# Layer one's output projection as seven-product pairs of row blocks, with row and weight sums in place

## What is computed

```
out = jnp.concatenate([y_mix, ym], axis=-1) @ w_out        # layer one: (tokens, 1536) @ (1536, 1024)
x = x + _rmsnorm(out, p['g_post'][l])
h = _rmsnorm(x, p['g_pre'][l + 1])                         # what layer two starts from
```

## Time and profile before

| | us |
|---|---|
| median of 3 runs (1755.45 to 1756.52) | 1755.72 |
| the profiled execution's own time | 1758.04 |
| its span in the trace | 1756.3 |
| PE busy | 1741.5 |
| DVE / ACT / POOL busy | 872.8 / 595.0 / 499.3 |
| A's output stage in the trace, 732.35 to 913.53 | 181.18 |

### The profile page before, as it was taken

How to read it: one execution, slowest core, us unless ns; L and a number is a source line. 1 busy time by engine, 2 the same in 40 slices (tenths; PEclk the granted TensorE clock), 3 DMA queues, 4 the chain that set the end, 5 groups by cost and what they waited for, 6 DMA issues and landing times.

```text
span 1756.3 us, 22816 instructions
## 1 busy us (share of the span) xinstructions
PE 1741.5 (99%) x8470; PEld 1353.8 (77%) x8470; DVE 872.8 (50%) x1801; ACT 595.0 (34%) x1445; POOL 499.3 (28%) x539
## 2 busy tenths in 40 slices
PE   9999999999999999999999999999999999999998
PEld 5577766888788888747558888888888888889643
DVE  0444423776666556451333443355335544565775
ACT  1421234564565234311221233432333234533312
POOL 0151100335232012410003543145414643122640
PEclk9999999999999999999999999999999999999999
DMA  8311111246755235541111111323123343745333
GB/s 271 138 61 66 66 45 50 55 151 158 230 171 166 85 100 164 178 147 48 50 58 57 41 48 45 99 88 96 50 73 117 97 148 109 266 146 181 132 108 110
DMA packets 149081, 196.25 MB, mean 112 GB/s; under 512 B 19083, under 2 KB 108171, under 8 KB 148834
## 3 DMA queue, kind: packets, MB, share of 16 engines
q1 hardware_dynamic: 140708, 174.58, 31.3%
q10 hardware_dynamic: 8262, 20.20, 3.3%
HBM read 156.97 MB, written 37.85 MB: 111 GB/s over the span
## 4 chain that ended last, share of the span: by engine, by line
PE 90%; DVE 3%; issue 3%; ACT 1%; DMA 1%; POOL 1%; SPq 0%; DVEq 0%; ACTq 0%; POOLq 0%
PE PS L3547 50%; PE PS L2289 7%; PE PS L2439 6%; PE PS L2079 3%; PE PS L575 3%; PE PS L401 3%; PE PS L2530 2%; PE PS L2115 2%; PE PS L2090 2%; PE PS L296 2%; PE PS L2112 2%; PE PS L925 1%; DVE WK L732 1%; PE PS L918 1%; PE PS L3445 1%
## 5 line engine op out<-in xcount | busy, mean ns | idle before, releaser
L3547 PE MATMUL PS<-HT,RING 128*128 128x258 f32 (+2 forms) x1776 | 445.6, 382 | 0.3 <-ACT WK L3637 0.3
L3547 PEld LDWEIGHTS PS<-HT,RING 128*128 128x128 f32 x1776 | 328.5, 190 | 48.0 <-issue 4.1
L3637 ACT ACTIVATE BIG<-PS 128x256 f32<-128x256 f32 (+2 forms) x140 | 53.7, 384 | 375.2 <-PE PS L3547 375.1
L3547 PE MATMUL PS<-BIG,RING 128*128 128x258 f32 (+1 forms) x656 | 159.7, 382 | 0.9 <-DVE BIG L3731 0.9
L3547 PEld LDWEIGHTS PS<-BIG,RING 128*128 128x128 f32 x656 | 123.0, 190 | 19.1 <-DVE BIG L3731 1.3
L3547 PE MATMUL PS<-BIG,WK 128*128 128x258 f32 (+1 forms) x448 | 113.7, 383 | 0.0
L3547 PE MATMUL PS<-HT,CST 128*128 128x256 f32 (+2 forms) x432 | 110.2, 382 | 0.1
L3547 PEld LDWEIGHTS PS<-BIG,WK 128*128 128x128 f32 x448 | 82.7, 190 | 14.0 <-issue 3.0
L3547 PEld LDWEIGHTS PS<-HT,CST 128*128 128x128 f32 x432 | 79.6, 190 | 11.4 <-DVE BIG L3736 0.9
L575 PE MATMUL PS<-WK,RING 128*128 128x344 f32 x288 | 84.3, 453 | 0.1
L3733 DVE TENSOR_TENSOR BIG<-BIG,PS 128x256 f32<-128x256 f32 (+1 forms) x70 | 29.5, 422 | 103.6 <-PE PS L3547 103.4
(11 more groups left out here) (455 smaller groups left out, 3270.6 us busy)
## 6 DMA issues: line engine op xcount, KB each, us to landing
RING<-in_w_in_a SPq DMA_DIRECT2D x14, 1024.0 KB, 6.7
WK<-in_cache_mem_kv SPq DMA_DIRECT2D x56, 256.0 KB, 5.6
RING<-in_w_kv_b SPq DMA_DIRECT2D x12, 1024.0 KB, 5.2
RING<-in_w_in_b SPq DMA_DIRECT2D x12, 1024.0 KB, 5.3
WK<-in_cache_win SPq DMA_DIRECT2D x40, 256.0 KB, 5.4
RING<-in_w_mkv SPq DMA_DIRECT2D x16, 512.0 KB, 4.9
BIG<-in_x_prompt SPq DMA_DIRECT2D x16, 512.0 KB
BIG<-sample_query SPq DMA_DIRECT2D x28, 256.0 KB, 5.8
```

What stands on the lines that cost most here:

```text
L3547: last = nc.tensor.matmul(PS[:, bank, 0:mid - lo], weight_block(u // 2, s, k), h_block(layer_of(u), u % 2, t, k), start=(k == 0 and j not ...
L3637: nc.scalar.activation(part(u, n2 if j == 0 else n1, lo, mid), PS[:, banks(u)[0], 0:mid - lo], ACT.Copy).then_inc(sig("projections_copied" ...
```

## The change

Layer one's output takes the form that layer two's has. `column_products`, `columns_turn`, `block_products` and `out_pe` go. Each of the four pairs takes seven products of six pieces x 512 columns; the first factor's blocks are the rows of the two token blocks (pieces 0 to 5 and 6 to 11), the second factor's are the weights (pieces 0 to 5 and 6 to 11, two halves of columns). The order of blocks becomes layer two's, with the sample block as number 4.

- Row sums S1 to S4 are made by DVE, mostly in place over the rows they come from (two instructions each, 16 sums).
- Weight sums: T3 and T4 by POOL, T1 and T2 by DVE, six instructions of 128x512 each, mostly in place.
- The results are summed by DVE with `pair_sum_dve` and copied by `pair_copy_act`, as in layer two.
- The sample block is computed by `sample_rows_pe` (12 pieces x 4 strips of 256 columns, bank 6).
- Turns of blocks 7 and 8 move into layer two's slots 3 and 6 (before: block 8's in slot 4); the T sums of layer two's second unit move from slots 5 to 7 to slots 7 to 9. Layer two's first unit waits for seven copied blocks and for each T sum where it needs it.

```diff
+        PAIR_ORDER_A = [(0, 0), (2, 0), (5, 0), (7, 0), (0, 2), (2, 2), (5, 2), (7, 2),
+                        (0, 4), (0, 1), (0, 3), (0, 5), (0, 6),
+                        (2, 1), (2, 4), (2, 3), (2, 5), (2, 6),
+                        (5, 1), (5, 4), (5, 3), (5, 5), (5, 6),
+                        (7, 1), (7, 5), (7, 3), (7, 4), (7, 6)]
...
+            out, x, y, op = {S3: (s3, a11, a21, ALU.subtract), S1: (a21, a21, a22, ALU.add),
+                             S2: (a11, a21, a11, ALU.subtract), S4: (a12, a12, a11, ALU.subtract)}[s]
+            for n in range(2):
+                last = nc.vector.tensor_tensor(out[n], x[n], y[n], op)
...
+        def weight_sum_a(engine, ops, t):
+            if t == T3:
+                engine.wait_ge(*product_done(UA - 1, NPROD - 1))
+                engine.wait_ge(sig("out_weights_loaded").sem, 80)
+                engine.wait_ge(sig("late_weights_loaded").sem, 128)
+            elif t == T1:
+                engine.wait_ge(*weights_a_ready(T3))
+                engine.wait_ge(sig("sample_rows_done").sem, 1)
+            elif t == T2:
+                engine.wait_ge(*weights_a_ready(T1))
+                engine.wait_ge(*pair_product_done("A", OUT_PAIRS[-1], 0))
+            elif t == T4:
+                engine.wait_ge(*weights_a_ready(T2))
+                engine.wait_ge(*pair_product_done("A", OUT_PAIRS[-1], 2))
+            x, y = {T3: (B22, T1), T1: (T1, B11), T2: (B22, T1), T4: (T2, B21)}[t]
+            for k in (0, 1, 5, 2, 3, 4):
+                if t == T4 and k == 2:
+                    engine.wait_ge(*pair_product_done("A", OUT_PAIRS[0], 4))
+                last = ops.tensor_tensor(weight_tile(t, k), weight_tile(x, k), weight_tile(y, k), ALU.subtract)
+            last.then_inc(sig("pair_weights_summed").up(), 1)
...
+        def out_a_pe(pe, free0, free1):
...
+            pair_product(pe, x, p2, 0, early)
+            pair_product(pe, x, p3, 0, early)
+            samples_turned_pe(pe, x)
+            pe.wait_ge(sig("late_weights_loaded").sem, 128)
+            for p in OUT_PAIRS:
+                pair_product(pe, x, p, 0, range(5, 6))
+            pe.wait_ge(sig("small_read").sem, SMP[x]["small"]["sp"])
+            sample_rows_pe(pe, x, range(8))
+            pe.wait_ge(sig("ym_ready").sem, 4)
+            for n, p in enumerate(OUT_PAIRS):
+                pair_product(pe, x, p, 2)
+                value(2 * n)
+                value(2 * n + 1)
+            pair_product(pe, x, p0, 4)
...
+            pair_product(pe, x, p1, 5)
+            block_turn(pe, x, 1)
+            pair_product(pe, x, p1, 6)
+            pair_product(pe, x, p2, 1)
+            pair_product(pe, x, p2, 4)
+            block_turn(pe, x, 2)
+            pair_product(pe, x, p2, 3)
+            block_turn(pe, x, 3)
...
+            pair_product(pe, x, p3, 4)
+            block_turn(pe, x, 6)
+            pair_product(pe, x, p3, 6)
...
+        def out_a_dve(dve, sample_out):
...
+            for n in range(4):
+                value(n)
+            weight_sum_a(dve, nc.vector, T1)
+            value(4)
+            value(5)
+            rows(p0, S3)
+            rows(p0, S1)
+            weight_sum_a(dve, nc.vector, T2)
+            value(6)
+            value(7)
+            rows(p0, S2)
+            rows(p0, S4)
...
+            pair(p1, C21)
+            h_copy_dve(dve, x, 1)
+            block_all_dve(dve, x, 2)
+            pair(p1, C12)
+            block_dve(dve, x, 3)
+            pair(p2, U2)
+            block_norm_dve(dve, x, 3)
+            row_sums_dve_a(dve, p3)
+            block_all_dve(dve, x, 4)
+            h_copy_dve(dve, x, 2)
...
+            h_copy_dve(dve, x, 6)
+            h_copied(dve, 7)
+            h_sum(dve, "B", 0, T1)
+            h_sum(dve, "B", 0, T2)
+            block_dve(dve, x, 7)
+            pair(p3, C12)
+            h_sum(dve, "B", 0, T3)
+            h_sum(dve, "B", 0, T4)
+            block_dve(dve, x, 8)
...
         def stage5_pool(pool):
+            weight_sum_a(pool, nc.gpsimd, T3)
             scale_pair(pool, PA)
             sum_pair(pool, PA)
+            weight_sum_a(pool, nc.gpsimd, T4)
             scale_pair(pool, PA + 1)
...
         def layer_b_dve(dve):
...
+                if x == 1:
+                    block_norm_dve(dve, "A", 7)
+                if x == 3:
+                    block_norm_dve(dve, "A", 8)
                 if x == 4:
+                    h_copy_dve(dve, "A", 7)
+                if x == 7:
                     h_copy_dve(dve, "A", 8)
+                    h_copied(dve, NB)
+                if 7 <= x < 10:
+                    for t in ((T1, T2), (T3,), (T4,))[x - 7]:
                         h_sum(dve, "B", 1, t)
```

More of the change, by code:

```diff
@@ L2350, in row_blocks @@
         def row_blocks(i):
-            first, second = (slice(BLOCKS["B"][j] * P, (BLOCKS["B"][j] + 1) * P) for j in (i + 1, i))
+            first, second = (slice(BLOCKS[j] * P, (BLOCKS[j] + 1) * P) for j in (i + 1, i))
             y, ym = tiles4(0, 1), tiles4(16, 1)
@@ L2429, in pair_product @@
+            u = BLOCKS[i + 1 if s in (A11, A12) else i]
             rows = slice(u * P, (u + 1) * P)
             for k in ks:
[L2431 to L2438 removed]
@@ L2439, in pair_product @@
-                last = nc.tensor.matmul(PS[:, bank, :], x, w, start=(k == 0 and j not in (2, 3, 6)), stop=(k == 3),
+                if x == "A":
+                    y, w = row_tile(i, s, k), weight_tile(t, k)
+                else:
+                    y = row_sum(i, s)[:, k] if s in (S1, S2, S3, S4) else c.src(k if s == A11 else 4 + k, rows.start, rows.stop)
+                    if t in (T1, T2, T3, T4):
+                        w = weight_sum(t)[:, k]
+                    else:
+                        w = c.piece(k if t == B11 else 4 + k)
+                        w = w[:, 512:D] if t == B22 else w[:, 0:512]
@@ L2440, in pair_product, with pair_copied @@
+                last = nc.tensor.matmul(PS[:, bank, :], y, w, start=(k == 0 and j not in (2, 3, 6)), stop=(k == nk - 1),
                                         skip_group_check=True)
-            if ks[-1] == 3:
+            if ks[-1] == nk - 1:
                 last.then_inc(sig("projections_done").up(), 1)
[L2444 to L2452, removed]
+        def pair_copied(x, i):
+            n = 2 * UA if x == "A" else 2 * NUNIT + len(OUT_PAIRS)
+            return sig("projections_copied").sem, n + OUT_PAIRS.index(i) + 1
@@ L2502, in sample_rows_pe, with sample_rows_bank @@
+        def sample_rows_bank(x):
+            return 6 if x == "A" else 7
+        def sample_rows_pe(pe, x, kts):
+            c = OUT[x]
+            if kts[-1] == c.kts - 1:
+                pe.wait_ge(sig("sample_out_read").sem, SMP[x]["order"] + 1)
+            for kt in kts:
                 for q in range(4):
-                    last = nc.tensor.matmul(PS[32 * q:32 * q + NS, 7, 0:256], c.src(kt, T, W),
+                    last = nc.tensor.matmul(PS[32 * q:32 * q + NS, sample_rows_bank(x), 0:256], c.src(kt, T, W),
@@ L2549, in build, with value @@
-        VALUE_SLOTS = {"A": {(0, 6): 0, (0, 7): 1, (0, 9): 2, (0, 10): 3, (1, 5): 4, (1, 6): 5, (1, 8): 6, (1, 10): 7}}
-        TURN_SAMPLES = {"A": 8}
-        def out_pe(pe, x, free0, free1, weights0, weights1):
-            c, order = OUT[x], SMP[x]["order"]
-            slots = VALUE_SLOTS[x]
-            def value(i):
-                def after(kt):
-                    if (i, kt) in slots:
-                        sample_values_pe(pe, x, slots[i, kt])
-                return after
-            def turns(at):
-                def after(kt):
-                    for i in at.get(kt, ()):
-                        block_turn(pe, x, i)
-                return after
-            early, late = range(c.early), range(c.early, c.kts)
-            own, cross = range(c.kts - H), range(c.kts - H, c.kts)
+        def out_a_pe(pe, free0, free1):
+            x = "A"
+            p0, p1, p2, p3 = OUT_PAIRS
+            def value(n):
+                sample_values_pe(pe, x, n)
+            early = range(5)
@@ L2578, in out_pe @@
-            ym = 0
-            pe.wait_ge(sig("ym_ready").sem, ym + 1)
-            pe.wait_ge(*weights1)
-            for i in range(2):
-                block_products(pe, x, i, late, value(i))
-            pe.wait_ge(sig("ym_ready").sem, ym + 4)
-            hold = turns({6: (0,), 11: (1,)})
-            last = value(2)
-            def both(kt):
-                last(kt)
-                if kt == TURN_SAMPLES[x]:
-                    sample_out_pe(pe, x)
-                hold(kt)
-            block_products(pe, x, 2, late, both)
```

493 lines of the change are left out of this document (272 added, 221 removed).

## The result

The changed kernel takes **1759.49 us** (median of 20 runs, 1757.96 to 1764.92), the kernel before 1756.43 (20 runs, 1754.94 to 1758.99). The ratio is 1.0019, with a 95% interval from 1.0012 to 1.0025: 3.1 us slower, a small change, but its interval lies wholly above 1. The forecast was 1.0 us faster. The profiled execution has a span of 1760.4 us and an own time of 1762.27.

What follows compares the result with a forecast made beforehand. TensorE (PE) was taken as the bound, busy 1741.5 of 1756.3 us. Its work falls 19.7 us, waits add 18.7, so 1.0 less: 1754.7 us, own range 1751 to 1758 (chance 0.50), stated range with rivals 1744.5 to 1761.

Steps and rivals of the forecast that it cites:

- PE's work: Layer one's output stage: 168.9 us of PE work removed, 150.0 added, 0.8 for shape changes, so 19.7 less.
- the values: Sample values late on DVE, which loses 13.4 us beside POOL; value 7 ready at 788.8, PE waits 7.9 us.
- U2 of the first pair: This sum comes about 0.4 us late, since two row sums before it run beside T4's second half.
- turn of block 3: PE waits 4.0 us for DVE's copy of block 2, which stands behind the sample block.
- layer two, slots 2 and 3: Start of layer two, from turn 6: DVE needs 14.8 us against PE's 10.4, a wait of 4.4.
- layer two, second unit: Block 8's copy and T1, T2 stand behind slot 6's sum: waits of 1.3 and 0.7, 2.0 us together.
- The clock falls in the pauses: Slower rival, chance 0.09: half clock behind two long pauses costs 5.2 us each, 10.3 more, 1765.0 us.
- row sums at half speed: Slower rival, chance 0.10: strided row sums take twice the time before value 7 and in stall 2, 6 more, 1760.7 us.
- DVE one for one with POOL: Side by side, each DVE instruction with two SBUF inputs starts about every 1.57 us and loses 0.95.
- eight sums at 0.4: At the values: POOL's sum of layer two's first weights, eight short instructions costing DVE 0.4 us each, put at 3.0.
- stall 2: PE's wait at the turn of block 3: DVE's 26.3 us against PE's 22.4, put at 4.0 us.
- The first rival: Faster, chance 0.31: DVE and POOL hardly meet, the values' wait and its 0.4 vanish, 9.3 us less, 1746.4.

Runs made afterwards that it cites:

- e7_u2_first: e5_both with layer two's start reordered (block 8's work and T4 later) and DVE summing U2 of the first pair ahead of two row sums: 1737.54 us, ratio 0.9883.
- e3_fill: Changed kernel with unused matmuls filling PE's pauses ahead of values 6 and 7 and of turn 3, waits kept: 1756.30 us, ratio 1.0002.
- e1_pool_first: Changed kernel with POOL scaling and summing layer two's first weights before T3, not between T3 and T4: 1749.39 us, ratio 0.9958.
- e2_copy_first: Changed kernel with DVE and ACT copying block 2 ahead of the sample block, not behind it: 1753.82 us, ratio 0.9988.
- e4_all_pool: Changed kernel with weight sums T1 and T2 moved from DVE to POOL, none left on DVE: 1763.46 us, ratio 1.0035.
- e5_both: Changed kernel with the edits of e1_pool_first and e2_copy_first together: 1743.07 us, ratio 0.9920.

## Why the prediction was wrong, point by point

e7_u2_first has the same order of work on PE as the changed kernel, with one short pause in the stretch that is compared. Laid beside it, the changed kernel's timeline shows what every pause really cost. The stage's first product and the sixth of layer two's second unit, in e7_u2_first:

```profile
731.79 3.70 PE L2542 MATMUL PS<-BIG 128*128 128x512 f32 x8 [0.51 <-DVE BIG L3877]
...
915.34 1.92 PE L3679 MATMUL PS<-BIG,RING 128*128 128x260 f32 x8
```

and slot 2's pause in the changed kernel:

```profile
911.60 1.89 PE L3682 MATMUL PS<-WK 128*128 128x256 f32 x8
914.88 1.99 PE L3682 MATMUL PS<-HT,RING 128*128 128x256 f32 x8 [1.39 <-ACT BIG L3772]
```

The same stretch takes 183.55 us in e7_u2_first, 206.21 in the changed kernel (732.92 to 939.13) and 202.98 before (732.35 to 935.33, the same product). In e7_u2_first 0.43 of it is idle. At slot 2 the changed kernel needs 3.28 us from start to start for what is 1.73 undisturbed: 1.55 lost, where the trace shows an idle time of 1.39. So each pause costs somewhat more than its idle time, here 0.16. That is how idle time is counted, and no cost of its own: undisturbed, eight such records are shown as 1.89 us long but the next start 1.73 us after them, so an idle time that is counted from their shown end leaves 0.16 out. The prediction's stalls were counted from start to start, and the last column is their like.

| | forecast, us | idle time shown | lost against e7_u2_first |
|---|---|---|---|
| PE's work | -19.7 | | -20.0 |
| the values (4 pauses) | 7.9 | 7.9 | 8.45 |
| U2 of the first pair | 0.4 | 0.75 | 0.8 |
| turn of block 3 | 4.0 | 3.95 | 4.1 |
| layer two, slots 2 and 3 | 4.4 | 3.2 | 3.75 |
| layer two, second unit (2 pauses) | 2.0 | 2.4 | 2.8 |
| clock behind the pauses | 0 | | 3.3 |
| sum | -1.0 | | +3.2 |

The last column is the growth of the distance between equal products of the two traces across each pause, the 0.5 us of e7_u2_first's own pause added at the second unit. PE's work is 202.98 less 183.0 (183.55 without that pause). The sum meets 206.21 - 202.98 = 3.23.

**The step that failed is the clock.** The sum had no term for it. "The clock falls in the pauses" stood as a rival with 0.09, on the ground that "no row shows a pause of this length, so nothing speaks for it but its absence". The mechanism is the rival's: long pauses at the last values and at turn 3, in places and of a total size that the sum had forecast, and the records behind them at the lower level. One detail differs. The rival had one pause of some 4 us before value 6; there were two, 2.59 before value 6 and 3.64 before value 7, and the clock fell within the second (1.00 still for the records of 785.66, which take 0.43). The chance was too low, because the same prediction forecast pauses more than twice as long as the longest that the earlier trace rows showed at 1.00; an untried range is no evidence for either side. Its price was too high: 5.2 us behind each pause, 10.3 in all and 1765.0, where 1.7 and 1.6 were measured. I had priced a whole product at half speed. In the changed kernel the granted clock is 1.00 again from 794.00, at the end of about these eight records, and part of its time at the lower level lay inside the pauses (0.56 in the stretch from 786.00, in which PE was busy for 0.66 us), where it costs nothing. By the right size the rival would have given 1754.7 + 3.3 = 1758.0. Shown by e3_fill, which filled the pauses and gave 3.2 back, and by e1_pool_first and e2_copy_first, each of which gave back its wait and the clock behind it. The waits came to 19.9 us rather than 18.7, and PE's work to 20.0 rather than 19.7. So of the 4.2 us between the forecast (1.0 less) and this stretch (3.2 more) 3.3 are the clock and 0.9 the rest. That 1759.49 lies inside the stated range of 1744.5 to 1761 is luck: its upper end was set by the row sums at half speed, which did not happen, and the clock was left out of it.

The Trainium skill, "TensorE: Matmul & The Clock Gate" (Part 1), has a TensorE that was idle go back to half rate. The windows at 0.56 to 0.61 in and behind the pauses agree, and e3_fill's 1.00 with the pauses filled agrees as well.

**PE's work: right.** 20.0 us less, forecast 19.7.

**The books of two runs.** Ten pauses show 18.3 us of idle time and cost 19.9. With the costs, e1_pool_first should give back 8.45 + 1.7 = 10.1 and gave 10.1, e2_copy_first 4.1 + 1.6 = 5.7 and gave 5.7 at the medians. That both close to 0.1 us is in part luck. In the profiled executions the same stretch is 9.1 and 6.5 us shorter than in the changed kernel (197.14 and 199.71), since the clock's cost behind the pause that stayed was not the same (last section), and in e2_copy_first the waits that stayed were some 0.5 us shorter.

**The values: right in size and cause.** DVE one for one with POOL, 13.7 us lost against 13.4. e1_pool_first takes POOL's scaling and sums away from beside them, and T4 then starts behind value 7; only T3 is left. DVE takes 29.5 us to the end of value 7 (748.72 to 778.26), of which 1.7 is a wait for a load, so it loses 3.0 in place of 13.7, and PE's wait is gone with DVE's own work unchanged: the meeting and not DVE's load makes the wait. Two slips in the working are too small to matter: eight sums at 0.4 are 3.2, not 3.0, and stall 2's 26.3 less 22.4 is 3.9, not 4.0. The step of the change behind it is that T3, which waits for a late load, stands at the head of POOL's queue and holds back work that was ready; e4_all_pool shows the converse, DVE with less work but more meetings being no sooner. The first rival (1746.4), in which the two hardly meet, falls for the changed kernel; e1_pool_first shows that an order of POOL's work was enough to have it and more.

The pairs cost slightly more than the forecast's 1.57 us: POOL's two take 3.51 and 3.43, so 1.72 to 1.76. The Trainium skill, "SBUF — State Buffer" (section "SBUF: two separate sides"), has either engine hold the shared port pair for its whole instruction; worked out from that, the estimate is 0.62 + 1.24 = 1.86. The measured 1.7 lies between 1.57 and this; the rule's direction holds and its size is somewhat too large here.

**The turn of block 3: right.** 3.95 us of idle time, behind DVE's copy (L2809), and the copy stood behind the sample block. e2_copy_first shows it: with the copy moved, the wait is gone.

**Layer two's start: right places, 0.7 too much at slots 2 and 3, 0.8 too little at the second unit.** The wait at slot 2 is on ACT's copy (1.39) and at slot 3 on U2 (1.83), as told.

**Row sums at half speed: did not happen.** DVE in the changed kernel, four row sums in eight halves, so 1.0 for a row sum, as costed:

```profile
858.02 4.08 DVE L2409 TENSOR_TENSOR BIG<-BIG 128x256 f32<-128x256 f32 x8
```

Of the 20 pair sums only U2 of the first pair made PE wait for its own sake, 0.75 where 0.4 was told, and T4 made nobody wait.

## What to carry to other kernels

Where a kernel has kept TensorE busy without a break, a new pause is to be priced with the clock behind it: here 1.6 to 2.5 us behind a pause of about 4 us, and 1.45 to 2.2 behind two of 2.6 to 4.4 with only a small job between. Work that DVE and POOL do side by side on SBUF is to be placed, not only counted: work of POOL that was ready, put ahead of work that waits for a load and so away from DVE's urgent values, was worth 10 us here with not an instruction less. Within one engine, the copy that another engine waits for goes ahead of the block that nobody waits for yet (5.7 us).

## What the runs showed that was not expected

**A short pause was followed by the lower clock too, once.** In the profiled execution of the changed kernel the clock fell a third time, far from the change, at the start of the mLSTM part of layer one. PE in the changed kernel:

```profile
307.75 0.70 PE L915 MATMUL PS<-WK 128*128 128x257 f32 x2 [1.91 <-DVE WK L987]
308.29 1.59 PE L925 MATMUL PS<-WK 128*128 128x257 f32 x4
309.67 1.06 PE L884 MATMUL PS<-BIG 128*128 128x128 f32 x4
```

and in e1_pool_first, with the same code there:

```profile
307.63 0.70 PE L915 MATMUL PS<-WK 128*128 128x257 f32 x2 [1.54 <-DVE WK L987]
308.17 1.03 PE L925 MATMUL PS<-WK 128*128 128x257 f32 x4
309.03 0.61 PE L884 MATMUL PS<-BIG 128*128 128x128 f32 x4
```

After a pause of 1.91 us four records take 1.38 us from start to start, after one of 1.54 us 0.86. But the length of the pause alone does not decide it. In e5_both, the same code with the same work of PE before it, the pause at this place is 2.15 us, longer than the 1.91, and the four records behind it take 0.86. Windows of the changed kernel and of e5_both:

```profile
300.00:310.00 10.00, 8.09 (x44) 6.12 (x43) 3.31 (x8) 5.29 (x12) 4.17 (x4) 0.93 0.69 254
```

```profile
300.00:310.00 10.00, 7.85 (x50) 6.16 (x50) 4.04 (x10) 5.13 (x11) 4.31 (x4) 1.00 0.83 259
```

In the other seven profiles this pause is 1.54 to 1.73 us and the clock stays at 1.00, as it does behind the pause of 1.83 us at slot 3 of layer two. What decided in the one case stays open. This third dip is part of why the profiled execution (1762.27) lies above the median. I take it for chance and for no part of the change's cost, since neither the code nor the wait there is the change's: the wait was 1.57 in the kernel before.

**The same pause does not always cost the same.** At turn 3 e1_pool_first pauses for 3.96 us as the changed kernel does for 3.95, but its turn and its four records behind it take 1.73 and 3.41 us (855.97, 857.70, 861.11) where 0.87 and 1.72 are undisturbed: 2.55 lost in place of 1.6. e4_all_pool loses 1.7 there. At the values e2_copy_first loses 1.45, the changed kernel 1.7 and e4_all_pool, with pauses of 2.74 and 4.36, 2.2. So about 1.5 to 2.5 us is the range of these profiles, one execution of each kernel.

**Short DVE instructions lose as much as long ones.** DVE in e4_all_pool, where POOL's T4 (789.50 and on) stands beside the row-sum halves of 256 columns:

```profile
788.22 6.24 DVE L2409 TENSOR_TENSOR BIG<-BIG 128x256 f32<-128x256 f32 x4
```

That is 1.56 each, where the undisturbed ones take 0.5 (above): 1.05 lost, as much as an instruction of 512 columns loses beside the same sums (1.66 to 1.7 for 0.62). In e1_pool_first two such halves at 784.91 take 3.05 us. Four at 778.26 take 4.10, since the first of them runs before T4 starts at 778.88. Beside POOL the price goes by the number of instructions, so the narrower form is the dearer one there.
